# Two input and weight buffers of a split-precision transformer kernel moved by 320 bytes along the partition

## The reference

```python
# first kind, twice                      # second kind, twice
h = rms_norm(x, g_mix_norm[l])           h = rmsnorm(x, norm1_g[l])
z = h @ w_in[l]                          x = x + hybrid_mixer(h, ...)   # two gated linear attentions,
...  # attention, spatial gating, pooling               # sparse attention, merge gates
x = x + mix @ w_out[l]                   h = rmsnorm(x, norm2_g[l])
h = rms_norm(x, g_ffn_norm[l])           x = x + swiglu(h, w_ffn_gate[l], w_ffn_up[l], w_ffn_down[l])
x = x + (silu(h @ w_gate[l]) * (h @ w_up[l])) @ w_down[l]
```

## The kernel before

| tensor | address | modulo 2048 |
|---|---|---|
| `h_hi` | 75136 | 1408 |
| `act_hi`, `act_lo` | 91520, 136576 | 1408 |
| `h_lo` | 195648 | 1088 |
| `w_hi`, `w_lo` | 212032, 220224 | 1088 |
| `ring`, `cst` | 32896, 45184 | 128 |

## Time and profile before

### The profile page before, as it was taken

How to read it: one execution, slowest core, us unless ns; L and a number is a source line. 1 busy time by engine, 2 the same in 40 slices (tenths; PEclk the granted TensorE clock), 3 DMA queues, 4 the chain that set the end, 5 groups by cost and what they waited for, 6 DMA issues and landing times.

```text
span 3460.1 us, 43641 instructions
## 1 busy us (share of the span) xinstructions
PE 3310.2 (96%) x15368; PEld 2560.1 (74%) x15368; DVE 1407.5 (41%) x2518; ACT 725.0 (21%) x1482; POOL 1856.5 (54%) x856
## 2 busy tenths in 40 slices
PE   6999999989999999988999999999998899999998
PEld 5678888768888788764766888878877466688886
DVE  4554430455540325845113444132485611244411
ACT  3321000331000223417101110022341710111001
POOL 3257777427777773010445777777300034577774
PEclk8999999999999999968999999999996899999998
DMA  2122222203223222110222322222211012232231
GB/s 107 49 78 94 92 96 92 73 31 106 95 93 97 85 86 67 44 37 1 67 79 86 99 97 91 97 85 88 70 41 43 1 61 79 86 100 96 91 97 61
DMA packets 71438, 263.02 MB, mean 76 GB/s; under 512 B 7920, under 2 KB 7920, under 8 KB 71152
## 3 DMA queue, kind: packets, MB, share of 16 engines
q1 hardware_dynamic: 71280, 260.98, 23.0%
HBM read 258.85 MB, written 2.10 MB: 75 GB/s over the span
## 4 chain that ended last, share of the span: by engine, by line
PE 63%; POOL 15%; issue 14%; DVE 5%; ACT 2%; POOLq 0%; DVEq 0%; DMA 0%; SPq 0%; ACTq 0%
PE bank L565 61%; POOL w_hi L1238 9%; POOL w_lo L1244 6%; PE bank L1129 1%; ACT arena L1662 1%; DVE arena L1705 1%; DVE arena L2221 1%; DVE rope L1702 0%; DVE arena L1702 0%; ACT arena L1651 0%; DVE arena L2061 0%; DVE rope L1705 0%; DVE rope L2281 0%; ACT act_hi L1368 0%; DVE h_lo L1729 0%
## 5 line engine op out<-in xcount | busy, mean ns | idle before, releaser
L1238 POOL TENSOR_TENSOR w_hi<-ring,cst 128x1024 fp32r<-128x1024 f32 x418 | 795.9, 1904 | 1512.2 <-PE bank L565 935.8
L1244 POOL TENSOR_TENSOR w_lo<-ring,w_hi 128x1024 fp32r<-128x1024 f32 x410 | 1016.1, 2478 | 32.2
L565 PE MATMUL bank<-h_hi,w_hi 128*128 128x512 f32 x2256 | 909.2, 403 | 2.1 <-DVE h_lo L1729 2.1
L565 PE MATMUL bank<-h_lo,w_hi 128*128 128x512 f32 x2256 | 894.1, 396 | 0.0
L565 PE MATMUL bank<-h_hi,w_lo 128*128 128x512 f32 x2256 | 889.3, 394 | 0.0
L565 PE MATMUL bank<-act_hi,w_hi 128*128 128x512 f32 (+1 forms) x1296 | 488.2, 407 | 17.7 <-DVE act_lo L1939 8.7
L565 PEld LDWEIGHTS bank<-h_hi,w_hi 128*128 128x128 f32 x2256 | 421.9, 187 | 108.5 <-issue 4.6
L565 PEld LDWEIGHTS bank<-h_hi,w_lo 128*128 128x128 f32 x2256 | 425.4, 189 | 102.7
L565 PEld LDWEIGHTS bank<-h_lo,w_hi 128*128 128x128 f32 x2256 | 424.4, 188 | 97.2 <-issue 1.4
L565 PE MATMUL bank<-act_hi,w_lo 128*128 (+1 forms) x1056 | 423.6, 401 | 0.0
L565 PE MATMUL bank<-act_lo,w_hi 128*128 (+1 forms) x816 | 323.5, 396 | 0.0
(11 more groups left out here) (230 smaller groups left out, 3012.7 us busy)
## 6 DMA issues: line engine op xcount, KB each, us to landing
ring<-wstream SPq DMA_DIRECT2D x480, 512.0 KB, 3.4
par<-params SPq DMA_DIRECT2D x5, 656.5 KB, 4.4
x<-xT SPq DMA_DIRECT2D x4, 512.0 KB, 6.3
outT<-h SPq DMA_DIRECT2D x4, 512.0 KB, 2.7
cst<-const SPq DMA_DIRECT2D x1, 1436.5 KB, 10.4
arena<-pos SPq DMA_DIRECT2D x1, 256.0 KB, 10.4
```

What stands on the lines that cost most here:

```text
L565: return pe.matmul(out, lhsT, rhs, start=start, stop=stop)
L1238: return po.tensor_tensor(out, a, C("ones")[:, 0:1].broadcast_to([P, n]), ALU.mult)
L1244: po.tensor_tensor(pair_[1], raw, pair_[0].bitcast(F32), ALU.subtract).then_inc(done.sem, 1)
```

## The change

A gap of 80 floats (320 bytes) is put ahead of the area of `h_lo`, so `h_lo`, `w_hi` and `w_lo` (and `low_part` in mixer 1) lie 320 bytes higher. `h_lo` is now at 195968, `w_hi` at 212352, `w_lo` at 220544, each 1408 modulo 2048. Every other tensor stays. All instructions, their order, their waits and their sizes are the same on every engine; only addresses differ.

```diff
@@ -104,7 +104,8 @@
         MIX = 26032
-        ARENA = MIX + ND * T + 4 * TILE
+        GAP = 80
+        ARENA = MIX + GAP + ND * T + 4 * TILE
@@ -114,7 +115,7 @@
-        sb("arena_gap", [P, MIX - (2 * FB + 3) * T])
+        sb("arena_gap", [P, MIX + GAP - (2 * FB + 3) * T])
@@ -159,7 +160,7 @@
-        low_part = arena[:, MIX:MIX + ND * T].rearrange("p (a b) -> p a b", a=ND)
+        low_part = arena[:, MIX + GAP:MIX + GAP + ND * T].rearrange("p (a b) -> p a b", a=ND)
```

## The result

| | before | changed |
|---|---|---|
| median, us | 3463.38 (4 runs, 3459.43 to 3467.61) | 3410.25 (4 runs, 3405.21 to 3413.80) |
| ratio, 95% interval | | 0.9845 (0.9825 to 0.9866) |
| profiled execution | 3461.91, clock 0.959 | 3405.21, clock 0.959 |

The change makes the kernel 53 us faster by the medians, 1.5%; the two profiled executions lie 56.7 apart. A second comparison, with five executions of the changed kernel against nine, gave 3409.5 against 3461.1, 0.9851 (0.9831 to 0.9871).

What follows compares the result with a forecast made beforehand. The prediction took TensorE to bound the kernel, its matmul period set by operand placement. Terms of 58.9 us, less 2, gave 57 off 3461.9, so 3405; with 4.4 for the runs' median, 3409, range 3398 to 3430.

Steps and rivals of the forecast that it cites:

- What bounds the kernel: Feed-forward stages: TensorE is the bound, waiting 0.5 us in a whole stage; the matmul period depends on where operands lie.
- The step: Long matmul stages: periods of 0.2285 to 0.2334 us fall to 0.2266, as in the early tiles in act_hi, operands at one offset.
- The sum: Whole kernel: terms of 58.9 us, less 2 for matmuls just behind a wait, give 57 us gained.
- feed-forward: Gate and up, 4224 matmuls, 28.7 us gained; down in four layers, 11.8 us together.
- Projections, merge and `w_out` of mixer 2: 1968 mixer 2 matmuls without TensorE gaps, 0.0068 us each: 13.4 us; w_out's act products fall under another term.
- Fillers: 576 matmuls between pieces of attention in mixer 2: 3.9 us at most, half counted, 2.0.
- Mixer 1: Part of act_hi and act_lo by w_hi and w_lo outside down, 2.0 us counted in all; mixer 1 nearly unchanged.
- `w_hi` as moving operand term: Matmuls with w_hi and w_lo as moving operand, many of 256 columns: 1.0 us gained.
- What a faster TensorE meets: POOL in feed-forward: its wait of 1.14 to 1.21 us a tile shrinks to about 1.0; nothing takes the gain back.
- The better mixed state only: Rival: long stages lose the 0.2334 state but stay at about 0.2287; gain 37 us, time 3429; chance 0.09.
- nothing: Rival: the two read streams don't touch, early tiles are fast for another reason; time stays 3466; chance 0.08.
- Slower: Rival: equal offsets collide, long stages fall into 0.24 us; 55 us lost, time 3521; chance 0.05.

Runs made afterwards that it cites:

- the fine map: Matmuls alone, none of the model's work, weights 0 to 512 bytes above the moving block in steps of 8: 226.7 ns at 0, 120, 256, 376, 512, elsewhere 228.3 to 234.4.

## Why the prediction was right

**What bounds the kernel**: right. TensorE's waits in a feed-forward stage stayed at 0.6 us, and of the 59.9 us by which its busy time fell 56.7 came off the span.

**The step**: right, with the number. It said that the offset modulo 512 or less counts, that the early tiles show what the long stages will do, and 0.2266; measured 0.2267 in gate and up, all four down stages and `w_out`. The experiments narrow it to the distance of weights and moving block modulo 256 at steps of 16 bytes and more. The absolute place, which the prediction took care to include, doesn't matter at 64 bytes and does at 16. It took the two periods of down for states that stay once entered, and the down stretches entered from different places, above, bear that out.

**The sum**: 57 forecast, 56.7 between the two profiled executions, but 53 between the medians. That 3409 met 3410.25 to about 1 us is luck: the start of the sum, 3466, lay 3 above the median of 3463.38, and the gain was 4 too large against the medians. By term: feed-forward 40.5 forecast, 38.2 measured. The prediction took 2 off its whole sum for matmuls near a wait. Of the missing 2.3, 0.6 are the step itself, 6.67 ns where 6.8 was counted and, in the second layer's down, 2.2 for 1.9; the rest, 1.7, is of that kind and lies in the first and last tiles of each stage. Behind the last wait of down the old kernel ran at 228.9 ns, where the sum counted 233.4. Projections, merge and `w_out` of mixer 2: 13.4 and 1.0 of the `w_out` part forecast, 13.4 measured. That this comes so close is luck in part: the first copy of the projections won 6.9 while its clock went from 0.97 to 1.00, the second lost 0.7 while its clock went from 0.99 to 0.97. Fillers: 2.0 forecast, 2.9 measured in the attention stages. Mixer 1: about 1, measured 2.8, one copy 2.9 and the other nothing. These last differences are of the size by which two executions of the changed kernel differ (3.3 us in one mixer 1), so they show nothing of the placement. The `w_hi` as moving operand term had the wrong sign for its 256-column part: the mean period of 384 such matmuls went from 115.7 to 119.9 ns, 1.6 us lost where up to 1.0 was to be gained.

**What a faster TensorE meets**: right; POOL's wait shrank from 1.14 to 1.21 to 1.02 to 1.07, as worked out.

**The rivals**: none came. *The better mixed state only* would have shown 0.2287; a period near it, 0.2288, does occur in gate and up, with the weights alone moved and at distance 128. The rival *nothing* is refuted with TensorE alone at work: 226.7 against 233.3 ns by distance. The Trainium skill, "TensorE: Matmul & The Clock Gate", Part 2, says that two independent read ports keep the weight load from taking read bandwidth from the running matmul; these two numbers don't agree with a load that costs the matmul nothing wherever it lies, though that it is bandwidth which is short isn't shown. *Slower* fell on the reason given against it: equal distance is the good case. The reason given for it was a misreading of the earlier trace rows: behind a moving `h_lo` the distances are 240 and 232 ns in turn, so the 0.24 is a place in a sequence of six and not the price of a pair.

## What to carry to other kernels

Where a stream of matmuls bounds a kernel, take the distance from start to start and compare it between stretches whose operands lie differently; 6.7 ns of 233 come to 1.5% of the time here, and the busy share doesn't show them. For fp32r products of 512 columns with 128 columns of weights, put moving blocks and weight blocks at addresses that agree modulo 256 bytes, low and high parts alike, at multiples of 32 bytes. A gap of 16 floats does what the one of 80 did.

## What was not expected of the hardware

- The pattern of periods has a memory: the same instructions at the same addresses ran at 228.9 or at 233.3 ns for over 100 us, by where the sequence ahead had ended. A small change ahead of a long stage could thus move the stage by 2%.
- Distance 120 and 376 are as good as 0; 8 and 248 are not (230.8 and 233.3).
- With 256 columns distance 0 is among the worst and 64 the best, where with 512 columns 0 is among the best and 64 has the common bad value, 233.3. The stretches of the fine map at 0, 32, 64 and 96 bytes:

```profile
1298.70 7.93 PE L135 MATMUL bank<-mov,wts 128*128 128x256 f32 x64 [0.19 <-DVE tick L127]
1306.83 7.83 PE L135 MATMUL bank<-mov,wts 128*128 128x256 f32 x64 [0.19 <-DVE tick L127]
1314.85 7.53 PE L135 MATMUL bank<-mov,wts 128*128 128x256 f32 x64 [0.19 <-DVE tick L127]
1322.57 7.78 PE L135 MATMUL bank<-mov,wts 128*128 128x256 f32 x64 [0.19 <-DVE tick L127]
```

  At 64 bytes it is 113.3 ns, at 0 it is 120.0. The kernel has 384 such matmuls, in six unbroken stretches. By an estimate from these two periods, 384 x 6.7 ns, this is 2 to 3 us of 3410; it wasn't tried.
- At the lower of the two clocks the placement costs nothing. In the kernel before, matmuls of 512 columns whose blocks lie 320 bytes apart stand 0.427 us apart at a granted clock of 0.50:

```profile
1180.70:1182.00 1.30, 1.30 (x5) 0.50 0.16 57
```
```profile
1180.65 0.63 PE L565 MATMUL bank<-w_hi,act_lo 128*128 128x512 f32 x1
1181.08 0.63 PE L565 MATMUL bank<-w_hi,act_hi 128*128 128x512 f32 x1
1181.51 0.63 PE L565 MATMUL bank<-w_lo,act_hi 128*128 128x512 f32 x1
```

  Worked out over all stretches at that clock where `w_hi` or `w_lo` is an operand of 512 columns, the distance is 426 to 427 ns in the kernel before, in the changed one and with gaps of 384 and 448 bytes. That is 512 columns at 1.2 GHz with nothing on top, so the gain stands only where the clock is full.
